# Layers of a two-model kernel joined: alternating semaphore sets in place of clears and barriers, openings, tails and norms interleaved

## The reference

```python
def first_block(x, c, ...):
    c_act = silu(c)
    for l in range(2):
        mod = c_act @ ada_w[l] + ada_b[l]                 # (1, 6 * 1024)
        sh1, sc1, g1, sh2, sc2, g2 = split(mod, 6)
        xm = rms_norm(x, norm_mix_w[l]) * (1 + sc1) + sh1
        q, k, v, u_pool, ga, gp = split(xm @ w_in[l])
        merged = sigmoid(ga) * attention(q, k, v) + sigmoid(gp) * pool(u_pool)
        x = x + g1 * (merged @ w_out[l])
        xf = rms_norm(x, norm_ffn_w[l]) * (1 + sc2) + sh2
        # 8 heads, 16 of 16384 experts each: rows of expert_u and expert_v are gathered
        x = x + g2 * peer_ffn(xf, w_query[l], sub_keys[l], expert_u[l], expert_v[l])
    return rms_norm(x, final_norm_w)

def second_block(x, positions, ...):
    cos, sin = rope_tables(positions)
    h = x
    for l in range(2):
        h = h + 0.5 * swiglu(rms_norm(h, ln_ffn1[l]), ffn1_w13[l], ffn1_w2[l])
        u = rms_norm(h, ln_mix[l])
        h = h + (gate1 * ssd_branch(u) + gate2 * mla_branch(u, cos, sin)) @ w_o[l]
        h = h + 0.5 * swiglu(rms_norm(h, ln_ffn2[l]), ffn2_w13[l], ffn2_w2[l])
    return h                                              # swiglu: (silu(x @ gate) * (x @ up)) @ w2
```

## Time and profile before

| | |
|---|---|
| device time, median of 3 runs | 3895.23 us (3890.38 to 3896.43) |
| the profiled execution: its own time, its span | 3899.72 us, 3897.7 us |
| granted clock of TensorE, mean | 0.957 of full speed |
| busy: PE, DVE, ACT, GpSimd | 85%, 63%, 37%, 32% of the span |
| first projection of first layer 0 starts | 56.09 us |
| first layer 1, its first projection | 1129.59 us |
| second layer 0, first FFN projection | 2218.04 us |
| second layer 1, first FFN projection | 3062.71 us |

### The profile page before, as it was taken

How to read it: one execution, slowest core, us unless ns; L and a number is a source line. 1 busy time by engine, 2 the same in 40 slices (tenths; PEclk the granted TensorE clock), 3 DMA queues, 4 the chain that set the end, 5 groups by cost and what they waited for, 6 DMA issues and landing times. The chain is left out here.

```text
span 3897.7 us, 53121 instructions
## 1 busy us (share of the span) xinstructions
PE 3328.7 (85%) x18864; PEld 2591.0 (66%) x18864; DVE 2452.5 (63%) x4646; ACT 1445.6 (37%) x2819; POOL 1233.8 (32%) x1160
## 2 busy tenths in 40 slices
PE   5897888877768978788887699999999899999899
PEld 4794433333247943333432499888899898888899
DVE  6776556655557765555565454868555456777554
ACT  3532222222135322222221344565444444555443
POOL 0124777777721247777777100000000000000000
PEclk9899999999999999999999899999999999999999
DMA  6577999999965779999999465434456454434454
GB/s 244 176 267 271 364 372 367 373 351 347 370 238 178 268 271 366 369 365 366 365 341 380 165 184 152 146 115 139 126 161 182 146 184 146 129 122 134 125 180 156
DMA packets 259598, 945.66 MB, mean 243 GB/s; under 512 B 29456, under 2 KB 29840, under 8 KB 258960
## 3 DMA queue, kind: packets, MB, share of 16 engines
q0 software_dynamic: 161280, 587.27, 40.4%
q1 hardware_dynamic: 98064, 355.01, 28.6%
HBM read 941.12 MB, written 1.05 MB: 242 GB/s over the span
## 5 line engine op out<-in xcount | busy, mean ns | idle before, releaser
L594 PE MATMUL M<-v_rows,diag 128*128 128x512 f32 x2048 | 1012.9, 636 | 321.7 <-DMA v_rows<-in_expert_v_dram,expert 215.9
L256 PE MATMUL G<-x_high,w_high 128*128 128x256 f32 x3280 | 967.6, 295 | 69.6 <-DVE x_low L866 19.0
L594 PEld LDWEIGHTS M<-v_rows,diag 128*128 128x128 f32 x2048 | 382.6, 199 | 943.1 <-issue 485.8
L238 DVE TENSOR_TENSOR w_low<-ring,w_high 128x1024 fp32r<-128x1024 f32 x560 | 689.8, 1234 | 473.9 <-ACT w_high L231 470.4
L259 PE MATMUL G<-x_high,w_low 128*128 128x256 f32 x3280 | 939.9, 287 | 0.0
L258 PE MATMUL G<-x_low,w_high 128*128 128x256 f32 x3152 | 905.1, 287 | 0.0
L980 DVE CUSTOM_DVE_ANT_0 u_rows<-u_rows,attn 128x1024 f32<-128x1024 f32 x512 | 611.4, 1223 | 353.5 <-DMA u_rows<-in_expert_u_dram,expert 351.9
L231 ACT ACTIVATE w_high<-ring 128x1024 fp32r<-128x1024 f32 x560 | 590.5, 1056 | 392.4 <-PE G L256 382.9
L256 PEld LDWEIGHTS G<-x_high,w_high 128*128 128x128 f32 x3280 | 642.7, 196 | 86.2 <-issue 58.8
L380 POOL DMA_INDIRECT u_rows<-in_expert_u_dram,expert x512 | 556.6, 1087 | 320.5 <-issue 151.8
L259 PEld LDWEIGHTS G<-x_high,w_low 128*128 128x128 f32 x3280 | 642.4, 196 | 0.0
(11 more groups left out here) (317 smaller groups left out, 4012.8 us busy)
## 6 DMA issues: line engine op xcount, KB each, us to landing
ring<-in_stream_dram SPq DMA_DIRECT2D x654, 512.0 KB, 3.6
ada_ring<-in_ada_stream_dram POOLq DMA_DIRECT2D x96, 512.0 KB, 5.1
ring<-in_ada_stream_dram SPq DMA_DIRECT2D x16, 512.0 KB, 7.3
u_rows<-in_expert_u_dram,expert POOLq DMA_INDIRECT x512, 6.2
v_rows<-in_expert_v_dram,expert POOLq DMA_INDIRECT x512, 6.3
const<-in_const_dram SPq DMA_DIRECT2D x1, 1096.5 KB, 7.3
x<-in_x_dram SPq DMA_DIRECT2D x1, 1024.0 KB, 5.4
out_dram<-x SPq DMA_DIRECT2D x1, 1024.0 KB, 3.9
```

The lines of the kernel that those rows point to most:

```text
L238: dve.tensor_tensor(T["w_low"][:, n % PARTS, :], T["ring"][:, chunk % slots, :], T["w_high"][:, n % PARTS, :].bitcast(F32), ALU.subtract). ...
L256: mm = pe.matmul(out, T["w_high"][:, n % PARTS, tile], high(k), start=(k == 0), stop=False)
L594: mm = pe.matmul(M[:, 2 * t + half, :], T["diag"][:, n % 4, :], T["v_rows"][:, n % SLOTS, half * 512:(half + 1) * 512], start=(h == 0 and ...
```

## The change

The clears between layers go. There are two sets of semaphores, `_a` and `_b`; layers take them in turn (first 0: a, first 1: b, second 0: a, second 1: b), and GpSimd clears the other set while a layer runs. A few semaphores count through the whole program (`run`, `rows`). The hardware loops over layers are written out. The two first layers are still a block each; both second layers lie in one block. In particular:

- **Opening.** `first_ada` and the loading block are now inside first layer 0. SP issues c, x, bias, par, const, final_w, positions, and once eight steps are done the first weight chunks; GpSimd issues all 16 ada chunks at once into the expert rows' place. DVE takes reciprocal and `x * rstd` in between, after the 13th step. Sums of ada go to columns of an M bank, not a G bank (`ada_full`, `ada_read`); the steps sit at other places (`ADA_STEPS`). First layer 1 makes only its own four parts: 32 steps and chunks in place of 48.
- **End of a first layer.** The sum of token half 0 is copied, transposed and added inside the last round; `next_x` and `next_mean` square the new x and take its mean half by half; root and reciprocal follow in the old layer's block. The next layer's par and its first ring chunks are loaded before the block ends. `rope_angles` runs on DVE after round 2 and the sines on ACT after round 4.
- **First to second block.** First layer 1 leaves `x_high_2`, `x_low_2`, which are the halves of x times final_w times ln_ffn1, with no norm in them. The first FFN starts on these; both means (of x^2 and of (final_w x)^2) follow its first projection (`first_means`), and the two reciprocal roots are multiplied in later. x itself is normalised inside the FFN, one tile for each pair.
- **FFN norms deferred.** In every FFN the inputs are the halves of x times the weight; DVE multiplies each gate bank by `rstd` (a new instruction for each pair), ACT takes silu in SBUF, and each output takes two DVE instructions in place of one. The mean of the next norm is taken tile by tile beside the output projections, two tiles behind (`mix_norm`, `ffn2_norm`, `out_norm`). `sqrt_table` loads the table ahead.
- **Second layer 0 to 1.** The halves, squares and all but two tiles of the mean of layer 1 are made beside the last output projections of layer 0, the ring goes on (`Place` shifts its slots).
- **Store.** x leaves tile by tile, each as soon as it is done.

```diff
-ADA_STEPS = {9: 0, 17: 1, 25: 2}
+ADA_STEPS = {9: 0, 20: 1, 28: 2}
+ADA_PARTS = ((0, 1, 2, 3, 4, 5, 0, 1), (2, 3, 4, 5))
...
@@ first_layer, sync
+            if opening:
+                sp.dma_start(T["c_in"][:, :], io["c"]).then_inc(run["c_loaded"], 16)
+                sp.dma_start(x[:, :, :], io["x"]).then_inc(run["x_loaded"], 16)
...
+                sp.wait_ge(sem["ada_step"], KD)
+                for chunk in range(RING):
+                    load_chunk(sp, T["stream1"], layer, CHUNKS_1, ring, sem["w_loaded"], chunk)
             load_weights(sp, T["stream1"], layer, CHUNKS_1, ring, sem["w_loaded"], sem["w_used"])
+            if not opening:
+                sp.wait_ge(run["cleared"], 1)
...
+            sp.wait_ge(g_full, g_peer(PEER_HEADS - 1) + 5)
+            sp.wait_ge(sem["u_used"], ROUNDS * TOPK)
+            if opening:
+                for chunk in range(RING):
+                    load_chunk(sp, T["stream1"], 1, CHUNKS_1, ring, nxt["w_loaded"], chunk)
+            else:
+                for chunk in range(RING_2):
+                    load_chunk(sp, T["stream2"], 0, CHUNKS_2, T["ring_2"], nxt["w_loaded"][:RING_2], chunk)
@@ first_layer, vector
+            def first_ada():
+                for n in range(2 * KD):
+                    dve.wait_ge(rows[("u_landed", "v_landed")[n // SLOTS]][n % SLOTS], 16)
+                    ada_step(dve, T, sem, n, T["ada_first"][:, n, :])
+                    if n == 3 * KD // 2:
+                        inverse_std(0)
+                        normalise(0)
...
+                    if r == ROUNDS - 1 and k == TOPK - SUB - 1:
+                        add_y(0)
@@ second_layer, tensor
+        def first_means(j):
+            if j == 0:
+                for part, tile in enumerate((xm, T["weighed_sq"])):
+                    for k in range(KD):
+                        pe.wait_ge((sem["sq_ready"], run["weighed_ready"])[part], k + 1)
+                        mm = pe.matmul(NORM[:, part * S:(part + 1) * S], T["ones_d"][:, :], tile[:, k, :],
+                                       start=(k == 0), stop=(k == KD - 1))
+                    mm.then_inc(sem["norm_full"], 1)
+        def rest_of_mean(j):
+            if j == 0:
+                for k in (KD - 2, KD - 1):
+                    pe.wait_ge(sem["sq_ready"], k + 1)
+                    mm = pe.matmul(NORM[:, 0:S], T["ones_d"][:, :], xm[:, k, :], start=False, stop=(k == KD - 1))
+                mm.then_inc(sem["norm_full"], 1)
+        def mix_norm(j):
+            if j >= 2:
+                norm_part("mix", 1, j - 2)
@@ second_layer, scalar, ffn
-                    copy_out(g0 + 2 * j, silu[:, j % 2, :], ACT.Silu)
+                evacuated(act, g_free, g0 + 2 * j)
+                act.activation(silu[:, j % 2, :], silu[:, j % 2, :], ACT.Silu).then_inc(sem["silu_ready"], 1)
@@ second_layer, scalar, opening of layer 0
+            act_halves.ahead(act, H_FFN1, 1)
+            for k in range(KD):
+                square(k)
+            act_halves.ahead(act, H_FFN1)
+            act_halves.ahead(act, H_FFN1 + 1)
+            root(0)
+            act.wait_ge(run["first_ms"], 1)
+            act.activation(std[:, :], ff[:, 0, :], ACT.Sqrt, bias=T["eps"][:, :]).then_inc(sem["std_ready"], 1)
@@ second_layer, vector, ffn
+                dve.wait_ge(g_full, g + 1)
+                dve.tensor_tensor(silu[:, j % 2, :], G[:, g % GB, 0:S], rstd[:, :], ALU.mult
+                                  ).then_inc(g_free[g % GB], 1)
+                if opening and i == 0 and j < KD:
+                    link(dve.scalar_tensor_tensor(out=x[:, j, :], in0=x[:, j, :], scalar=T["final_w"][:, j:j + 1],
+                                                  in1=T["rstd_ssd"][:, :], op0=ALU.mult, op1=ALU.mult))
...
-                    dve.scalar_tensor_tensor(out=x[:, j, :], in0=G[:, g % GB, 0:S], scalar=0.5,
+                link(dve.tensor_tensor(silu[:, j % 2, :], G[:, g % GB, 0:S], rstd[:, :], ALU.mult))
+                dve.scalar_tensor_tensor(out=x[:, j, :], in0=silu[:, j % 2, :], scalar=0.5,
@@ second_layer, sync
+            for k in range(KD):
+                evacuated(sp, g_free, H_FFN2_OUT + k)
+                sp.dma_start(io["out"][:, k, :], x[:, k, :]).then_inc(run["stored"], 16)
@@ program
-                with nc.Fori(0, depth) as layer:
-                    clear()
-                    first_layer(nc, layer, T, sem)
-                clear()
-                final_norm(nc, T, sem)
+        for layer in range(DEPTH):
+            first_layer(nc, layer, io, T1, sets[layer][0], rows, run,
+                        sets[1][0] if layer == 0 else sets[0][1])
+        second_layers(nc, io, T2, [sets[0][1], sets[1][1]], run)
```

2176 lines of the change are left out of this document (1178 added, 998 removed).

## The result

The changed kernel took 3813.59 us, median of four runs (3806.96 to 3819.46), against 3893.55 for the kernel before beside it (four runs, 3890.38 to 3896.43): ratio 0.9775, 95% interval 0.9754 to 0.9795. The profiled execution has a span of 3811.8 us and a time of 3813.55: 85.9 us less span than before, where 73.6 was forecast.

What follows compares the result with a forecast made beforehand. PE sets the pace in the FFN and loses time at the seams, where one chain stands alone. Savings of 10.8 + 9.9 + 25.3 + 16.6 - 4.8 + 10.8 + 1.8 + 3.2 = 73.6 give 3821.6 us; 8 in 10: 3807 to 3838.

Steps and rivals of the forecast that it cites:

- D: Second layer 0 to 1: mean tiles between output projections, projection 0 follows at once; saves 16.6 us, bounds 18 and 12.
- E2: Before the second FFN, twice: the seam of 12.94 us becomes 7.6; saves 5.4 each, 10.8 us; bounds 7 and 2 each.
- C: First to second block: norm, clears and rope leave the path; saves 25.3 us, between 20.6 and 29.6.
- A: Opening: first projection at 45.3 against 56.09 us, saves 10.8; 14 if DVE alone sets the pace, 5.5 if other loads lead.
- Rival 1: Opening gains nothing because x, const and ring loads share the DMA engines with the ada chunks; time 3832 us, chance 0.09.
- B: First layer 0 to 1: seam of 26.3 us shortens, saves 9.9; 5.0 with a loop-turn start, 10.9 with a hidden one.
- E1: Before mixing, twice: gap of 6.58 us becomes 9.0 in all; loses 2.4 each, 4.8; bounds 0 and 4 each.
- Ada in layer 1: First layer 1 makes two parts less of ada, one of them in PE's path; saves 1.8 us, bounds 0 and 3.6.
- FFN steady state: New DVE instruction of 0.42 us in each pair costs nothing over 88 pairs; low half ready 2 us before PE wants it.
- Rival 3: Fewer stalls: ACT and DVE reach chunk 4 in time, mixing seams lose nothing; 12.8 us more saved, 3809, chance 0.08.
- Rivals 1 and 2: The second: seams between blocks cost 5.9 us like a loop's turn, not about 1, at two starts; 3831, chance 0.12.
- Rival 4: FFN pairs: the deferred norm holds up the weights, 1.23 us a pair, 108 over 88 pairs; time 3930, chance 0.03.

Runs made afterwards that it cites:

- experiment 1: Changed kernel rerun against the kernel before: 3905.08 against 3959.19 us, ratio 0.987; also the kernel before with its layer loops written out, single run 3945.05 us.
- experiment 3: Changed kernel with constants, final weights and positions loaded after the eighth ada step: single run 3917.63 us; first projection at 42.43, against 45.2 to 46.9.
- Experiment 4: Changed kernel with weight halves reordered around the two norms at the second block's first FFN: single run 3896.42 us; 144.88 against 148.55 to 148.86 in that piece.
- Experiments 5 and 6: Changed kernel, single runs: low halves before mixing moved behind reciprocal and scaling, 3907.79 us; all mean tiles moved behind the last output product, 3886.82 us.
- experiment 7: Against the kernel before: changed kernel unedited 0.9803, row buffers aligned by 32 bytes 0.9798, three small moves together 0.9794; kernel before shifted 32 bytes 0.9987.
- the waiting kernel: Changed kernel with both second FFNs waiting for their norm's reciprocal before projection 0: 3836.33 us, against 3912.21 for the kernel before.
- the first comparison: Changed kernel against the kernel before, four runs each: 3813.59 against 3893.55 us, ratio 0.9775.
- experiments 1 and 2: The second: changed kernel with two all-engine barriers behind each first layer, single run 3885.37 us; 15.95 instead of 15.29 between the first layers.
- 3 to 6: Changed kernel with constants late, halves reordered at first FFN, low halves later before mixing, mean tiles last: 3917.63, 3896.42, 3907.79, 3886.82 us; kernel before 3974.37.
- 8: Changed kernel with second FFNs waiting for their norm, 3836.33 us; with the deferred product four or eight times a pair, 6.37 or 8.20 us a pair against 5.70.

## Why the prediction was right in its direction, and which step failed

Direction and mechanism stand: PE's time at the seams is what fell. The saving was under-forecast, and at the second FFN by more than its stated bounds allow.

The step that failed is an overlap. The forecast put ACT's table load for silu, 1.28 us, in line behind the norm's product, and so a stall of 1.1 us at D and at each E2, and one of 4.7 at C. In the trace ACT loads that table while DVE is still at a chunk's low half or the reciprocal, and then waits for the product: 2.11 us at D and at both E2, 1.44 us at C. The load costs the path nothing; there is no stall at D and E2, and 3.27 at C. Of the miss of 12.3 us that is 3.3 and up to 0.6 at C. The other misses are terms of the sum that were mis-sized or put at nothing, and luck. Piece by piece:

- *E2, second FFN, twice: 10.8 forecast (at most 14), 19.0 in the profile.* These 8.2 are two thirds of the miss of 12.3. The seam itself gave 13.9 (twice 13.03 - 3.99 - 2.1 for five mean tiles at 0.42), 3.1 over the forecast: 2.2 are the two stalls, and the 0.9 are mainly the mean tiles, which took 3.0 us for eight where 3.6 was forecast. 2.5 us are products of the FFN: PE's pitch there fell from 2.88 to 2.85 us a projection, which no step of the forecast held. The other 2.6 are the mixing stage, and they are luck: its piece in layer 0 took 552.39 us, one other profile with the same code there has 552.28, and seven have 556.5 to 557.9. What sets the two lengths apart is PE's clock, below. By the two kernels' profiles in experiment 1, E2 gives 15.1 and not 19.0.
- *A, 10.8, measured 9.7.* The middle of three mechanisms was the right one, with the chunks 1 to 2 us later than forecast; experiment 3 shows the shared engines as the cause. Rival 1 falls, though its mechanism is there, at 3.6 us rather than all of 10.8.
- *B, 9.9, measured 11.0.* The seam between blocks costs little; experiment 1 shows the turn's 3.8.
- *C, 25.3, measured 25.9.* The stall was 3.27 rather than 4.7, by the table load; of the 1.4 only 0.6 shows in the sum. Experiment 4 takes all but 0.87 of the stall away.
- *D, 16.6, measured 17.9.* 20.0 less 2.1 for the mean tiles; no stall behind the norm, with 1.1 forecast.
- *E1, -4.8, measured -3.2.* Each loses 2.1 and gets 0.5 back. Experiments 5 and 6 confirm both parts.
- *Ada in layer 1, 1.8, measured 3.7; end, 3.2, measured 3.8.* The first lies in the scatter of that piece: 283.4 to 292.8 in the profiles of the changed kernel and its variants.
- *FFN steady state, 0, measured 0.* Right, for a wrong size: the margin was put at 2 us and is 0.70 behind the product. One product was hidden, and by these numbers one more would be; of a third, part would not.

These sum to 87.8; the stretch before the first expert sum of layer 0 was 0.6 longer and the rounds 1.3, which leaves 85.9.

The clock of the mixing stage, in windows of 20 us from 100 us behind the first dt product of layer 0, in the changed kernel's first profile and in the one of experiment 7:

```profile
2470.00:2490.00 20.00, 16.74 (x136) 15.00 (x135) 11.12 (x18) 13.16 (x29) 0.00 (x0) 1.00 0.33 106
```

```profile
2552.00:2572.00 20.00, 16.74 (x114) 15.48 (x113) 9.06 (x16) 10.71 (x23) 0.00 (x0) 0.83 0.27 82
```

PE is busy for the same 16.74 us and gets through 136 products with a granted clock of 1.00, and through 114 with 0.83. Its two waits for DVE there are the same in both (2.12 and 3.26 us). In the whole piece PE is without products for 24.7 us in the changed kernel's first profile and 24.4 in that of experiment 1, and busy for 527.7 and 532.2. Over the whole piece the clock was at its lower level for 16.3 us in the three stages of 552.3 to 552.4 us, and for 27.1 to 29.0 in those of 556.5 to 558.1.

Rival 3 (fewer stalls) was half true: of its 12.8 us, 3.3 came at D and E2, 1.4 at C and 1.6 at E1. Rivals 1 and 2 fall. Rival 4 did not happen, but stands nearer than its 0.03 told.

Not settled: why the rounds take 1513 to 1518 us in some groups and 1557 to 1611 in others, and whether the 1600.3 against 1557.6 of experiment 1 is more than chance: the profiles of experiment 7 show no such difference between the kernels. In the five short profiles PE is without products for 305 to 322 us of the rounds and its clock is low for 95 to 136 us; in the long ones it is 346 to 384 and 164 to 270. Which of the two leads is not shown. Open too is why the clock falls in one mixing stage and not in the other with the same waits, and why the pitch of products in FFN 2 fell; the same code has 2.88 in layer 0 and 2.85 in layer 1 of the waiting kernel.

## What to carry to other kernels

At a seam between stages, cost the chain that stands alone (last sum, norm, halves, first product) and the clock that PE loses over it; barriers are cheap beside it (some 0.35 us each at the end of a block here) and a loop's turn is not (3.8). Before a table load goes into the chain, see whether its engine stands idle ahead of it. Moving a product behind the matmul pays where its result is a factor of each column, but follow the ring of waits through the engines, not their busy share: here DVE was idle a third of the time with 0.70 us of slack a pair. Judge a change at seams by pieces of the timeline: the expert rounds moved the total by half of the gain within one group of runs, and by as much as the gain between groups.

## What the runs showed of the hardware

- The same 32 expert rounds took 1514 and 1516 us in the first comparison, 1558 to 1600 in experiments 1 and 2, 1586 to 1611 in 3 to 6, 1584 to 1593 in 7 and 1513 to 1518 in 8, on the chip of 1 and 2 again; a shift of their buffers by 32 bytes made no difference to be told from this.
- A loop's turn cost 3.8 us on the path, twice in one profile; two barriers of all engines behind a block 0.7, and 0.8 where other profiles scatter by 0.6.
- No drain was seen behind a table load: the root starts 1.29 us behind the start of a load of 1.28. ACT loaded silu's table while it would have waited for DVE anyway, at no cost.
- The granted clock was 0.50 from 20 to 46 us in the opening, after PE had been busy for 5.2 of the 15 us before; in the waiting kernel 0.5 and 2.4 us without products were followed by a projection at 0.50 and 0.21 us a product rather than 0.12.
- The same mixing stage took 552.3 to 552.4 us with the clock at its lower level for 16.3 us, and 556.5 to 558.1 with 27 to 29 us, with the same waits of PE.
